# Two-layer hybrid encoder on one core: attention's small products side by side, next head's loads spread, projections in rows

## The reference

```python
for l in range(DEPTH):                                   # DEPTH = 2
    h = x @ w_in[l]                                      # 1024 -> 2048 columns
    aq, ak, av, bq, bk, bv, cx = jnp.split(h, IN_OFFSETS, axis=-1)
    oa = swa_sink_attention(aq, ak, av, a_sink[l], bias_a)       # 6 heads, band of 2 chunks of 64, a sink
    ob = diff_attention(bq, bk, bv, lam, ..., bias_table_b)      # 6 heads, two softmax maps each: p0 - lam * p1
    oc = multiscale_pool(cx, c_pool_w[l], c_scale[l])            # windowed means, 4 groups, small product
    mixed = jnp.concatenate([oa, ob, oc], axis=-1) @ w_o[l]
    x = layer_norm(ALPHA * x + mixed, ln1_g[l], ln1_b[l])
    x = layer_norm(ALPHA * x + conv_gated_mlp(x, w_up[l], conv_w[l], conv_b[l], w_down[l]), ...)
    # gated mlp: h = x @ w_up (1024 -> 5632), causal convolution of 3 taps, silu(g) * u, then @ w_down (2816 -> 1024)
```

## Time and profile before

| what | us |
|---|---|
| median of 3 runs | 2650.52 (2649.97 to 2664.36) |
| the profiled execution's own time | 2659.14 |
| its span | 2657.2 |
| PE busy | 2489.5 (94%) |
| POOL busy | 1626.1 (61%) |
| DVE busy | 1418.5 (53%) |
| ACT busy | 830.3 (31%) |
| granted TensorE clock, mean | 0.971 |

### The profile page before, as it was taken

One profiled execution on the slowest core, in us unless ns is written; L12 is line 12 of the kernel. 1 busy time (PEld: TensorE's weight loads), 2 busy tenths in 40 slices (PEclk: granted clock), 3 DMA queues, 4 the chain that ended last, 5 costly groups with the idle time before them and its releaser, 6 DMA issues.

```text
span 2657.2 us, 32612 instructions
## 1 busy us (share of the span) xinstructions
PE 2489.5 (94%) x11608; PEld 1998.2 (75%) x11608; DVE 1418.5 (53%) x2845; ACT 830.3 (31%) x1711; POOL 1626.1 (61%) x2884
## 2 busy tenths in 40 slices
PE   8988898999999999899999999989999999998996
PEld 6766676877877778677777887767777777887885
DVE  4345635555655385145556375165655637466556
ACT  1124314444442121035453121044444411321221
POOL 6842365555655778666566677654555567786873
PEclk9988898999999999999999999989999999999998
DMA  6632223332322223433232323522332222333331
GB/s 193 190 84 76 79 77 102 84 96 76 95 72 69 90 72 118 115 84 104 86 90 73 95 80 103 137 82 83 88 88 76 72 72 80 109 106 99 99 95 64
DMA packets 347281, 249.17 MB, mean 94 GB/s; under 512 B 37291, under 2 KB 306927, under 8 KB 347119
## 3 DMA queue, kind: packets, MB, share of 16 engines
q1 hardware_dynamic: 321792, 211.01, 26.7%
q10 hardware_dynamic: 25327, 36.07, 5.2%
HBM read 226.32 MB, written 20.71 MB: 93 GB/s over the span
## 4 chain that ended last, share of the span: by engine, by line
PE 75%; DVE 14%; ACT 4%; DMA 3%; issue 2%; POOL 1%; ACTq 1%; SPq 0%; DVEq 0%
PE psum L769 45%; PE psum L996 13%; PE psum L864 6%; PE psum L819 3%; PE psum L797 3%; PE psum L850 2%; DVE conv L1402 2%; DVE room L1271 2%; DVE conv L1380 1%; ACT conv L1188 1%; DVE x_res L1551 1%; DMA w_raw<-in_w_in 1%; DVE hid L1407 1%; POOL w_lo L748 1%; DVE x_res L1586 1%
## 5 line engine op out<-in xcount | busy, mean ns | idle before, releaser
L745 POOL CAST w_hi<-w_raw 128x256 fp32r<-128x256 f32 x1440 | 562.2, 432 | 994.7 <-DMA w_raw<-in_w_up 527.0
L748 POOL TENSOR_TENSOR w_lo<-w_raw,w_hi 128x256 fp32r<-128x256 f32 x1440 | 1083.7, 783 | 0.0
L769 PE MATMUL psum<-x_hi,w_hi 128*128 128x512 f32 x2048 | 847.9, 414 | 40.2 <-POOL w_lo L748 19.8
L769 PE MATMUL psum<-x_hi,w_lo 128*128 128x512 f32 x2048 | 815.4, 398 | 0.0
L769 PE MATMUL psum<-x_lo,w_hi 128*128 128x512 f32 x2048 | 814.5, 398 | 0.0
L769 PEld LDWEIGHTS psum<-x_hi,w_hi 128*128 128x128 f32 x2048 | 394.9, 193 | 135.6 <-POOL w_lo L748 24.3
L996 PE MATMUL psum<-hid,w_hi 128*128 128x512 f32 x1408 | 452.2, 402 | 17.7 <-DVE x_res L1586 12.4
L769 PEld LDWEIGHTS psum<-x_hi,w_lo 128*128 128x128 f32 x2048 | 394.0, 192 | 87.7
L769 PEld LDWEIGHTS psum<-x_lo,w_hi 128*128 128x128 f32 x2048 | 395.0, 193 | 73.2 <-issue 1.7
L1380 DVE SCALAR_TENSOR_TENSOR conv<-psum,prm_all,conv 128x511 f32<-128x511 f32 x176 | 131.8, 749 | 463.5 <-ACT conv L1188 463.4
L996 PEld LDWEIGHTS psum<-hid,w_hi 128*128 128x128 f32 x1408 | 254.9, 190 | 76.3 <-DVE hid L1407 13.0
(11 more groups left out here) (126 smaller groups left out, 2265.8 us busy)
## 6 DMA issues: line engine op xcount, KB each, us to landing
w_raw<-in_w_up SPq DMA_DIRECT2D x176, 512.0 KB, 3.8
w_raw<-in_w_down SPq DMA_DIRECT2D x88, 512.0 KB, 3.7
w_raw<-in_w_in SPq DMA_DIRECT2D x36, 512.0 KB, 3.9
w_raw<-in_w_o SPq DMA_DIRECT2D x32, 512.0 KB, 4.1
qk_scratch<-stage_qk SPq DMA_DIRECT2D x48, 256.0 KB, 3.5
q_stack<-qk_scratch ACTq DMA_DIRECT2D x72, 128.0 KB, 2.7
k_stack<-qk_scratch ACTq DMA_DIRECT2D x36, 256.0 KB, 4.8
w_raw<-in_w_in SPq DMA_DIRECT2D x16, 384.0 KB, 3.5
```

Of the source, the lines that this page charges most:

```text
L745: nc.gpsimd.tensor_copy(w_hi[:, slot, cut], w_raw[:, slot, cut]).then_inc(s["w_high"], 1)
L748: i = nc.gpsimd.tensor_tensor(w_lo[:, slot, cut], w_raw[:, slot, cut], w_hi[:, slot, cut].bitcast(F32), ALU.subtract)
L769: mm = nc.tensor.matmul(o, w, v[:, k, :], start=(k == 0 and w is wh and v is x_hi[h]), stop=(k == KT - 1 and w is wl))
```

## The change

It has four parts.

- **A step of attention.** `attend` gives one step per unit in the order AV of unit u-4, AT of unit u-3, A1 of unit u, AW of unit u-1, then (half 1, kind b) A2 of unit u. Before, the order was A1(u), AW(u-1), AV(u-3), A2(u), AT(u-2), each with feed-forward work before it. The shares of A1, AT and AW are now 0, and the step's share stands on AV (and an own one on A2).
- **Loads spread.** ACT issues two of the six loads of the next head's stacks after the exponential of each of the first three units of kind a, and the table's load with the last two.
- **Rows.** Layer 1's projections and all output projections stand in a row: share 0 for all but the first event of the row (`in_row`, `begins_row`), and `merge` begins a row only where no feed-forward tile is in use in part.
- **Banks of the values.** Layer 1's `V` results go to banks d0 to d3 instead of `sb` and `tb`, and are copied out in four instructions of 512 columns (two on DVE, two on ACT) instead of two of 1024.

No product and no transfer is added or left out.

```diff
 def attend(l, h):
-    for u in range(UNITS + 3):
+    for u in range(UNITS + 4):
+        if u >= 4:
+            out.append(("AV", l, h, u - 4))
+        if 3 <= u < UNITS + 3:
+            out.append(("AT", l, h, u - 3))
         if u < UNITS:
             out.append(("A1", l, h, u))
         if 1 <= u <= UNITS:
             out.append(("AW", l, h, u - 1))
-        if u >= 3:
-            out.append(("AV", l, h, u - 3))
         if u < UNITS and h == 1 and unit_of(u)[0] == "b":
             out.append(("A2", l, h, u))
-        if 2 <= u < UNITS + 2:
-            out.append(("AT", l, h, u - 2))
     return out
...
+def in_row(e):
+    return e[0] == "O" or (e[0] in ("P", "V", "W", "CW", "AS") and e[1] == 1)
+def begins_row(e):
+    return (e[0] == "O" and e[3] == 0) or (e[0] == "P" and e[1] == 1 and e[3] == "c0")
 def share(e):
+    if in_row(e) and not begins_row(e):
+        return 0.0
+    if kind == "A1" and e[3] == 0:
+        return 5.0
+    if kind == "AV":
+        h, u = e[2], e[3] + 4
+        wide = width_of(h, min(u, UNITS - 1))[1] / HALF
+        return 1.6 + 1.2 * wide if u < UNITS and not (h == 1 and unit_of(u)[0] == "b") else 1.2 + 1.2 * wide
+    if kind == "A2":
+        return 0.8 + 1.2 * width_of(e[2], e[3])[1] / HALF
+    if kind in ("A1", "AT", "AW"):
+        return 0.0
...
 def merge(main, other, until=1.0):
-    due = 0.0
+    due, last, downs = 0.0, None, 0
     for e in main:
-        while n < len(other) and due + share(other[n]) * each <= had + 1e-9:
+        if last is not None and last[0] == "D":
+            downs += 1
+        whole = last is None or (last[0] != "U" or last[5] == PARTS - 1) and downs % 4 == 0
+        last = e
+        while n < len(other) and due + share(other[n]) * each <= had + 1e-9 and (whole or not begins_row(other[n])):
...
     def attention(e):                                   # on ACT
-                    load = last_of_head(e)
-                    if load and load[0] == "stacks":
-                        load_head(h, load[1])
-                        load_near(h, load[1])
-                    elif load:
-                        load_table(h, load[1])
+                    n = u % (2 * HT) - HT
+                    if n >= 0 and head_of_b(u) + 1 < B_HEADS and n < 3:
+                        load_head(h, head_of_b(u) + 1, range(2 * n, 2 * n + 2))
+                        if n == 2:
+                            load_near(h, head_of_b(u) + 1)
+                    elif n == HT - 1 and last_of_head(e):
+                        load_table(h, last_of_head(e)[1])
```

More of the change, by code:

```diff
@@ L280, in signals @@
             return {"v_used": 1}
-        if e[1] == 0:
-            return {f"d{n}_{what}": 1 for n in range(4) for what in ("full", "free")}
-        return {"sb_full": 1, "sb_free": 1, "tb_full": 1, "tb_free": 1}
+        return {f"d{n}_{what}": 1 for n in range(4) for what in ("full", "free")}
     if kind in ("W", "O"):
@@ L362, in place_banks @@
             keys = [e[:5]]
-        elif kind == "V" and e[1] == 0 and e[3] == 0:
+        elif kind == "V" and e[3] == 0:
             keys = [("V", *e[1:3], t) for t in range(HT)]
@@ L442, in ends @@
             return tile, "v_used"
-        return tile, f"d{BANK[tile]}_full" if tile[1] == 0 else "tb_full"
+        return tile, f"d{BANK[tile]}_full"
     if kind == "P" and tile[3] == "aq0" and tile[1] == 1:
@@ L777, in values @@
                 n = tile_in(e)
[L778 to L781, removed]
+                outs = [d_bank(BANK["V", l, h, t]) for t in range(HT)]
                 if i == 0:
@@ L784, in values @@
                         pe.wait_ge(s["xl"], after(normed(l, h), "xl"))
[L785 to L790, removed]
+                    for bank in range(4):
+                        take(e, f"d{bank}")
                 for t in range(HT):
@@ L923, in _ @@
                         v = ("V", e[1], e[2], HT - 1)
-                        for name in (f"d{BANK[v]}_free",) if e[1] == 0 else ("sb_free", "tb_free"):
-                            pe.wait_ge(s[name], after(v, name))
+                        for t in range(HT):
+                            bank = f"d{BANK['V', *e[1:3], t]}_free"
+                            pe.wait_ge(s[bank], after(v, bank))
                     scores(e)
@@ L1022, in constants, with load_head @@
                 act.dma_start(m_b, mask_b[:, :]).then_inc(s["small"], 16)
-            def load_head(h, head):
+            def load_head(h, head, parts=range(6)):
                 p, j = divmod(head, 2)
[L1027 to L1032, removed]
+                for n in parts:
+                    v, g = divmod(n, 3)
+                    stack, cut = ((q_stack, slice(h * HALF, (h + 1) * HALF)), (k_stack, slice(0, (h + 1) * HALF)))[v]
+                    src = qk_dram[v, p, STACKED[v][g], 2 * j * QK:2 * (j + 1) * QK, cut]
+                    act.dma_start(stack[QK * g:QK * (g + 1), :, 0:cut.stop - cut.start].bitcast(F32),
+                                  src.rearrange("(m r) c -> r m c", m=2)).then_inc(s["stacked"], 16)
             def load_near(h, head):
@@ L1125, in _ @@
                     l, h, i = e[1:]
-                    if i == HT - 1:
-                        t = HT * h
-                        if l > 0:
-                            act.wait_ge(s["tb_full"], after(e, "tb_full"))
-                            nc.scalar.copy(v_all[:, t + 2:t + 4, :],
-                                           wide("tb").rearrange("p (t c) -> p t c", t=2)).then_inc(s["tb_free"], 1)
+                    if i == HT - 1 and l > 0:
+                        for t in (2, 3):
+                            n = BANK["V", l, h, t]
+                            act.wait_ge(s[f"d{n}_full"], after(e, f"d{n}_full"))
+                            nc.scalar.copy(v_all[:, HT * h + t, :], d_bank(n)).then_inc(s[f"d{n}_free"], 1)
                 elif kind == "AL":
```

28 lines of the change are left out of this document (9 added, 19 removed).

## The result

| what | us |
|---|---|
| the change, median of 4 runs | 2572.28 (2565.77 to 2579.62) |
| before, median of 4 runs | 2652.55 (2649.97 to 2664.36) |
| ratio | 0.9685, interval 0.9653 to 0.9717 |
| profiled execution, its span | 2579.62, 2577.7 |

A forecast was written before the change was run, and what follows sets the result against it. PE, busy 2489.5 of 2657.2 us, was taken as the bound. The terms -10 - 16 - 20 - 9 + 4 + 8 + 3 = -40 gave 2619 us for a profiled execution, 2611 for the median; range 2583 to 2648.

The forecast's parts named there:

- Products side by side: Attention's small products: joining AV to AT, and AT to scores, saves spacing; -10 us, bounds -5 and -17.
- Rows and slots: Projections: no feed-forward tile holds a slot in a row, so PE's waits for POOL's weights go; -16 us.
- Loads and AV: Attention: spread loads and AV a block later cut AV's waits for ACT; -20 us, bounds -34 and 0.
- Clock: Behind removed waits: about ten stretches at 1.2 GHz go; -9 us, bounds -17 and 0.
- Start of attention: Attentions beside feed-forward work: first scores wait for DVE, partly offset by a vanished 7.35 us wait; +4 us.
- Norms behind a row: LI events directly follow the eighth O, with less covering work before LO; +8 us, bounds +2 and +12.
- DVE against POOL in rows: In rows, DVE instructions with two SBUF inputs stand behind POOL, delaying result banks; +3 us, bounds 0 and +8.
- waits did not come back elsewhere: Rival for feed-forward parts: later waits for DVE eat the gain of terms 3 and 4; 2640 us, chance 0.2.
- transfers did not limit a row: Rival for rows: 16 tiles make SP's queue late, term 2 and its clock share vanish; 2631 us, chance 0.08.
- the clock rival: Attention's 50 blocks of small products could each cost a clock fall of 1.7 us; 2696 us, chance 0.1.
- The rival's own row: Clock rival's evidence: a stretch of small products alone, PE never idle, is followed by clock 0.50 at 44.80.

The follow-up runs named there:

- the order alone: Kernel before with only the new order within a unit (shares, loads, projections as before): ratio 1.0012 (0.9987 to 1.0038).
- the last run: The change plus covered attention starts, transposes filling PE's waits, rows beginning anywhere and layer 1's values on score banks: 2550.65 us, ratio 0.9579 to before.

## Why the prediction was wrong

The direction was right and the size was half. By its steps:

1. *Products side by side*, -10: measured on the spacing of the dense products around them about -9. Right.
2. *Rows and slots*, -16: the 16.7 us of the earlier trace rows are gone; with the values' 1.2 and one new wait of 3.3 in the last part, -17.7 in the whole. At its old place the tile aq2 of the earlier trace rows follows aq1 without a gap. Right. Rows alone brought 26, the clock with it.
3. *Loads and AV*, -20: AV's waits fell by 28.4 us in all. The gross terms -13 - 8 - 5 = -26 were right in sum, though the last had a wrong reason: not "a block behind" but the dense work gathered between the scores and AV. The +6 booked against them hardly came: 1.3 us for the stacks, and no wait in AV's place.
4. *Clock*, -9: **the step that failed most.** The count held: 21 stretches at 1.2 GHz between 156 and 2253 us before, 12 now, so nine fewer for my ten. The size did not. The stretches are 5.7 us long in the mean before and now, and each costs up to half of that, 2.8 us; I had taken 0.9 apiece, half of the 1.7 that a single stretch of 3.4 us in the earlier trace rows could cost. 9 x 2.8 = 26 us, beyond even my bound of -17. In the second profile of the change it is 22 (14 stretches, 75 us), and by the mean clocks of all runs, 162 to 166 us before and 106 now, 28 to 30 at most.
5. *Start of attention*, +4: half 0's first scores and AT in layer 1 wait 7.5 us (4.9 before), layer 0's half 1 6.4 (3.0), and the last attention 9.0 (10.1): +5. Right. But the sum was right by other parts than mine. The wait of 7.35 us in the earlier trace rows was no accident of one execution: with the loads alone and with the order alone DVE's same subtraction stood 8.53 and 8.57 us at the same place. Each kernel with the old shares of attention has a score wait of 7.3 to 7.6 us at the start of one of layer 1's attentions, and of those with the new shares only the last run has one, of 5.4.
6. *Norms behind a row*, +8: LI waits 2.5 us for its issue and LO 3.3 instead of 7.4, in all about -1. The cost that I had put at 8 did not come; why LO gained was not tested.
7. *DVE against POOL in rows*, +3: 2.8 us, four waits of 0.7 for `stage_qk`. Right.

Sum with what was measured: -9 - 18 - 28 - 26 + 5 - 1 + 3 = -74; of the remaining 6, about 5 are score waits in mid-attention that I had not costed (from 420 to 2250 us, away from the starts: 5 us before, none now). Of the 40 us missed, 17 are the clock, 15 the costs of steps 3 and 6 that never came, and 8 lie in AV's waits and the rest.

The rivals: waits did not come back elsewhere (idle time fell by 46 us over the whole span), transfers did not limit a row, and the clock rival is refuted for attention's blocks: in the feed-forward parts the twelve longest of them that hold no wait, 3.0 us each, stand in the trace at full clock with no fall behind, and 34 transposes in 3.40 us keep it at 1.00. The rival's own row was right all the same: the block of products of 32 rows does precede a fall, as told above, but the change moved no such block, and what sets it apart was not tested. The Trainium skill, "TensorE: Matmul & The Clock Gate", Part 4, says that transposes don't count as PE being busy in the way other products do; for the fp32 transposes of this kernel these rows disagree as far as holding the full clock goes, and the measurement decides. Whether transposes would also raise it from 0.50 no row here shows.

**Idle time and clock together.** Over the eleven profiles here whose PE is not kept busy artificially, from 76 to 148 us of idle time (the sum of PE's gaps), each us of idle goes with 1.0 us at 1.2 GHz (straight line, correlation 0.92). And among runs of one and the same kernel, each us more at 1.2 GHz goes with 0.52 us more of time (70 runs of the changed kernel and the twelve others above, each against its kernel's mean; correlation 0.80), which is the half that I count it at. So a us of wait removed went along with about 1.5 us of time; that it caused them is an estimate from these two lines, not the result of a run. Rows, steps and loads alone give 26, 40 and 27 us, 94 by the medians, for the 80 of the whole change; for steps and loads the square of AV's waits shows the overlap, 16 and 17.5 us alone and 28 together.

## What to carry to other kernels

Where PE is the bound and its clock is below 1, cost a wait at its length and then half of the low-clock stretch behind it, read from the trace as long as it really is: here up to 2.8 us each, more than many of the waits themselves. One profile's low-clock time is one draw; take the mean clock of several runs. Before costing a new order as "later", write both orders out as sequences: a loop rotated by one step may give the same list, and all that changes is where the other work lies. And a start at which a pipeline is not yet full needs its own cover: one line in the table of shares, for three units of each attention, brought 32 us on top of 80.

## What the runs showed of the hardware

DVE's instructions with two inputs in SBUF can stand while several POOL instructions go by, not one. In the change, at the start of layer 1's first attention:

```profile
1100.36 1.43 POOL L772 CAST w_hi<-w_raw 128x256 fp32r<-128x256 f32 x4
...
1100.99 3.67 DVE L1315 SCALAR_TENSOR_TENSOR room<-room,ust 128x128 f32<-128x128 f32 x1
1101.75 2.76 POOL L775 TENSOR_TENSOR w_lo<-w_raw,w_hi 128x256 fp32r<-128x256 f32 x4
...
1104.72 0.47 PE L867 MATMUL psum<-ident,room 128*128 128x128 f32 x1 [3.47 <-DVE room L1315]
```

An operation of 128 columns takes 3.67 us (0.35 at the median of its kind) and ends at 1104.66, 0.15 us behind POOL's run of eight pieces (1101.75 + 2.76 = 1104.51); PE pays 3.47 us. That POOL is the cause is argued from this coincidence and the 8.62 us of the earlier trace rows; no run took POOL's work away.

The cost of issuing a transfer isn't constant: the same three `k_stack` loads at the same place took 3.16 us to issue in the kernel with the order alone and 1.41 with steps and shares (rows above). Spread, two loads delay a copy by 0.17 us.
